# A hybrid diffusion block on one core: layer norms in two parts, context tokens first

## What is computed

```python
def half_ffn(x, shift, scale, gate, w_in, w_out, g, b):
    h = modulate(x, shift, scale)                    # x * (1 + scale) + shift
    a, u = jnp.split(h @ w_in, 2, axis=-1)           # (1024, 2 * 2816)
    y = (jax.nn.silu(a) * u) @ w_out                 # (2816, 1024)
    return layernorm(ALPHA * x + 0.5 * gate * y, g, b)
```

## Time and profile before

| | |
|---|---|
| three runs | 3256.19, 3259.68, 3264.73 us, median 3259.68 |
| profiled execution | 3258.92 us, its span 3257.2 us |
| busy: PE, PEld, DVE, ACT, POOL | 93%, 76%, 49%, 26%, 7% of the span |
| mean granted TensorE clock | 0.969 |
| DMA | 269 MB, mean 83 GB/s |

### The profile page before, as it was taken

One profiled execution on the slowest core, in us unless ns is written; L12 is line 12 of the kernel. 1 busy time (PEld: TensorE's weight loads), 2 busy tenths in 40 slices (PEclk: granted clock), 3 DMA queues, 4 the chain that ended last, 5 costly groups with the idle time before them and its releaser, 6 DMA issues.

```text
span 3257.2 us, 41934 instructions
## 1 busy us (share of the span) xinstructions
PE 3040.4 (93%) x16507; PEld 2489.4 (76%) x16507; DVE 1582.5 (49%) x2391; ACT 842.5 (26%) x1262; POOL 237.8 (7%) x351
## 2 busy tenths in 40 slices
PE   5999999999976989999999899999996998899997
PEld 2588888877843768888887788888865897688785
DVE  3434344445456464343434644444354887454544
ACT  0411111124244141111112411111143665322221
POOL 1000000000010001010100000000001653000000
PEclk8999999999988999999999999999998999999998
DMA  7344432201121224343420222212111110133330
GB/s 284 104 146 138 131 114 65 65 27 52 52 69 53 65 78 155 116 154 117 154 91 26 65 65 64 59 60 61 39 47 46 28 26 14 52 116 90 90 92 38
DMA packets 292648, 269.32 MB, mean 83 GB/s; under 512 B 31111, under 2 KB 257263, under 8 KB 292432
## 3 DMA queue, kind: packets, MB, share of 16 engines
q1 hardware_dynamic: 269936, 188.95, 19.5%
q0 software_dynamic: 21760, 76.03, 6.7%
q10 hardware_dynamic: 864, 3.15, 0.3%
HBM read 262.85 MB, written 5.24 MB: 82 GB/s over the span
## 4 chain that ended last, share of the span: by engine, by line
PE 86%; DVE 6%; ACT 5%; issue 1%; DMA 1%; POOL 1%; SPq 0%; ACTq 0%; DVEq 0%; POOLq 0%
PE PSALL L1912 25%; PE PSALL L1913 24%; PE PSALL L1914 24%; PE PSALL L1833 2%; PE PSALL L2009 1%; PE PSALL L2260 1%; ACT H L810 1%; PE PSALL L2245 1%; PE PSALL L1875 1%; ACT HHI L813 1%; PE PSALL L2124 1%; DVE RSTD L1447 1%; ACT SQ L883 1%; PE PSALL L2099 1%; DVE X L1452 1%
## 5 line engine op out<-in xcount | busy, mean ns | idle before, releaser
L1912 PE MATMUL PSALL<-HHI,WHIA 128*128 128x512 f32 (+1 forms) x1520 | 536.6, 353 | 48.0 <-DVE HLO L1335 39.9
L1913 PE MATMUL PSALL<-HLO,WHIA 128*128 128x512 f32 (+1 forms) x1520 | 527.8, 347 | 0.0
L1914 PE MATMUL PSALL<-HHI,WLOA 128*128 128x512 f32 (+1 forms) x1520 | 527.0, 347 | 0.0
L1912 PE MATMUL PSALL<-HHI,WHIB 128*128 128x512 f32 (+1 forms) x1488 | 512.0, 344 | 10.8 <-DVE WLOB L1238 10.8
L1913 PE MATMUL PSALL<-HLO,WHIB 128*128 128x512 f32 (+1 forms) x1488 | 512.0, 344 | 0.0
L1914 PE MATMUL PSALL<-HHI,WLOB 128*128 128x512 f32 (+1 forms) x1488 | 511.2, 344 | 0.0
L1386 DVE SCALAR_TENSOR_TENSOR X<-PSALL,GATE,X 128x512 f32<-128x512 f32 (+1 forms) x616 | 376.1, 633 | 242.1 <-PE PSALL L1914 239.6
L1912 PEld LDWEIGHTS PSALL<-HHI,WHIA 128*128 128x128 f32 x1520 | 290.5, 191 | 113.3 <-issue 40.6
L1914 PEld LDWEIGHTS PSALL<-HHI,WLOA 128*128 128x128 f32 x1520 | 291.1, 192 | 35.6
L1912 PEld LDWEIGHTS PSALL<-HHI,WHIB 128*128 128x128 f32 x1488 | 281.9, 189 | 45.3 <-issue 8.5
L1913 PEld LDWEIGHTS PSALL<-HLO,WHIA 128*128 128x128 f32 x1520 | 291.8, 192 | 31.5
(11 more groups left out here) (265 smaller groups left out, 4279.9 us busy)
## 6 DMA issues: line engine op xcount, KB each, us to landing
RAW<-in_ffn_w_in_dram SPq DMA_DIRECT2D x176, 512.0 KB, 4.2
ADA<-in_ada_w_dram POOLq DMA_DIRECT2D x144, 512.0 KB, 4.9
RAW<-in_ffn_w_out_dram SPq DMA_DIRECT2D x88, 512.0 KB, 3.5
RAW<-in_ev_w_in_dram SPq DMA_DIRECT2D x20, 512.0 KB, 4.2
WRAW<-in_mla_w_q_up_dram SPq DMA_DIRECT2D x16, 288.0 KB, 3.0
RAW<-in_ev_w_out_dram SPq DMA_DIRECT2D x8, 512.0 KB, 4.8
RAW<-in_mla_w_in_dram SPq DMA_DIRECT2D x8, 512.0 KB, 4.2
RAW<-in_mla_w_out_dram SPq DMA_DIRECT2D x8, 512.0 KB, 4.6
```

The source lines that it names most:

```text
L1912: te.matmul(out, w_hi, x_hi(k), start=(k == 0), stop=False)
L1913: te.matmul(out, w_hi, x_lo(k), start=False, stop=False)
L1914: x = te.matmul(out, w_lo, x_hi(k), start=False, stop=(k == ks - 1))
```

## The change

1. `ORDER = {2: (1, 0), 1: (0,)}`: in a norm over both kinds the context is part a = 0, the latents part a = 1; h, residual and all counts follow.
2. `last_down`: the last down projection takes the eight context chunks, then the eight latent chunks, through other PSUM banks. The sums of a chunk (`sum_chunk`) stand two chunks later, and the context's variance after latent chunk 4.
3. `first_pair`: A and B of the next stage together. Chunk by chunk over the context: half 0 of A and of B; then the latents' variance; then half 1 over the context; then A's latents (both halves for each chunk as it comes), then B's.
4. `next_unit`: B's weights are split ahead of the norm's end, as A's.
5. `even_out` and `odd_out` replace `project` for the output projections, with sums between their products; in `even_out` units 2 and 3 take the context first.
6. The tables of coefficients (`tables`) go into the last FFN loop body; the SP queue's wait ahead of the rope tables now names the count of the norm before.

```diff
 # ScalarE, layernorm (S is 2 with context, 1 without)
+            if nxt:
+                next_unit(nxt, "A")
+            mean(0)
+            for m in range(KC):
+                square(0, m)
+            if nxt:
+                next_unit(nxt, "B")
+            root(0)
+            if name == "final":
+                return
+            if S == 2:
+                for m in range(3):
+                    h(0, m)
+                mean(1)
+                for m in range(KC):
+                    if m + 3 < KC:
+                        h(0, m + 3)
+                    square(1, m)
+                root(1)
+            for m in range(KC):
+                h(S - 1, m)
...
 # VectorE
+        def ctx_end(name):
+            for m in range(3, KC):
+                norm(name, 2, 0, m)
+                ln_low(name, 2, 0, m - 2)
+                if m >= 5:
+                    center(name, 2, 1, m - 5)
+            for m in (6, 7):
+                ln_low(name, 2, 0, m)
+                center(name, 2, 1, m - 3)
+            for m in range(5, KC):
+                center(name, 2, 1, m)
+        def ln_end(name, S):
+            a = S - 1
+            inverse(name, S, a)
+            norm(name, S, a, 0)
+            for m in range(KC):
+                if m + 1 < KC:
+                    norm(name, S, a, m + 1)
+                ln_low(name, S, a, m)
...
 # VectorE, end of an ffn
-            for e in range(KC * S):
-                accumulate(FI - 1, e)
+            next_unit(nxt, "A")
+            for m in range(KC):
+                last_chunk(1, m)
+            last_chunk(0, 0)
+            for m in range(4):
+                center(then, 2, 0, m)
+            last_chunk(0, 1)
+            for m in range(4, KC):
+                center(then, 2, 0, m)
+            for m in (2, 3, 4):
+                last_chunk(0, m)
+            next_unit(nxt, "B")
+            last_chunk(0, 5)
+            inverse(then, 2, 0)
+            last_chunk(0, 6)
+            for m in range(3):
+                norm(then, 2, 0, m)
+            ln_low(then, 2, 0, 0)
+            last_chunk(0, 7)
+            ctx_end(then)
...
 # VectorE, end of ev_out
+            for m in range(4, KC):
+                out_chunk("ev_out", 2, 1, 1, m, 4)
+            next_unit("ffn1", "A")
+            out_chunk("ev_out", 2, 1, 0, 4, 5)
+            for m in range(KC):
+                center("ln1", 2, 0, m)
+            out_chunk("ev_out", 2, 1, 0, 5, 6)
+            next_unit("ffn1", "B")
+            inverse("ln1", 2, 0)
+            for m in range(3):
+                norm("ln1", 2, 0, m)
+            out_chunk("ev_out", 2, 1, 0, 6, 5)
+            ln_low("ln1", 2, 0, 0)
+            out_chunk("ev_out", 2, 1, 0, 7, 6)
+            ctx_end("ln1")
...
 # TensorE, last_down
+                for m in range(KC):
+                    if m >= 4:
+                        te.wait_ge(evac, e0 + m - 3)
+                    chunk(1, m, last_bank(1, m))
+                    if m >= 2:
+                        sum_chunk(then, 2, 0, m - 2, e0 + m - 1)
+                for m in range(KC):
+                    if m >= 2:
+                        te.wait_ge(evac, e0 + KC + max(0, m - 3))
+                    chunk(0, m, last_bank(0, m))
+                    if m == 0:
+                        for k in (6, 7):
+                            sum_chunk(then, 2, 0, k, e0 + k + 1)
+                    if m >= 2:
+                        sum_chunk(then, 2, 1, m - 2, e0 + KC + m - 1)
+                    if m == 4:
+                        variance(then, 2, 0)
+                for m in (6, 7):
+                    sum_chunk(then, 2, 1, m, e0 + KC + m + 1)
...
 # TensorE, first_pair; columns() waits for h_lo chunk by chunk, at chunk 0 of part 0 for both slots' lo_done
+            if S == 2:
+                columns(0, [(slot, 0) for slot in "AB"])
+                if ln != "h0":
+                    variance(ln, 2, 1)
+                columns(0, [(slot, 1) for slot in "AB" if halves[slot] > 1])
+            for slot in "AB":
+                columns(S - 1, [(slot, half) for half in range(halves[slot])])[slot].then_inc(pe[slot], done[slot])
...
 # TensorE, even_out (after units 0 and 1)
+            for n, slot in enumerate("AB"):
+                te.wait_ge(evac, p.evac + 4 * (n + 1))
+                for half in range(2):
+                    x = unit_product("ev_out", slot, p.q + 4 + 2 * n, half, 1, order)
+                x.then_inc(pe[slot], 1)
+                for m in range(0, 4) if n == 0 else (4, 5):
+                    sum_chunk("ln1", 2, 0, m, p.evac + (8 if m < 4 else m + 5))
+            unit_product("ev_out", "A", p.q + 4, 0, 0, order).then_inc(pe["A"], 1)
+            for m in (6, 7):
+                sum_chunk("ln1", 2, 0, m, p.evac + m + 5)
+            for m in (0, 1):
+                sum_chunk("ln1", 2, 1, m, p.evac + 8)
+            unit_product("ev_out", "A", p.q + 4, 1, 0, order).then_inc(pe["A"], 1)
+            for m in (2, 3, 4):
+                sum_chunk("ln1", 2, 1, m, p.evac + (8 if m < 4 else 13))
+            variance("ln1", 2, 0)
+            unit_product("ev_out", "B", p.q + 6, 0, 0, order).then_inc(pe["B"], 1)
+            sum_chunk("ln1", 2, 1, 5, p.evac + 14)
+            unit_product("ev_out", "B", p.q + 6, 1, 0, order).then_inc(pe["B"], 1)
+            for m in (6, 7):
+                sum_chunk("ln1", 2, 1, m, p.evac + m + 9)
```

More of the change, by code:

```diff
@@ L457, in down_bank, with last_bank, stat_bank @@
         return PS[6 + m % 2][:, 0:LAT] if s == 0 else PS[5][:, CTX * (m % 2):CTX * (m % 2) + CTX]
+    LAST_CTX, LAST_LAT = (1, 2, 4, 5), (6, 7, 2, 1)
+    def last_bank(s, m):
+        return PS[(LAST_LAT if s == 0 else LAST_CTX)[m % 4]][:, 0:SEGS[s][1]]
+    STAT_BANKS = {"ln0": (3, 0), "ln1": (7, 6), "ln2": (3, 0), "ln3": (3, 0), "ln4": (6,), "final": (0,)}
+    def stat_bank(name, s):
+        return PS[STAT_BANKS[name][s]][:, 0:SEGS[s][1]]
     block = stack.enter_context(nc.Block())
@@ L857, in body @@
                     split_hi(slot, half, p.q + j, i, free_value(slot, i + d))
-            body(0, first=True)
+            silus("A", 0)
+            for slot, d, half, j in ffn_halves(False)[2:]:
+                split_hi(slot, half, p.q + j, 0, free_value(slot, d))
             if ada:
@@ L1006, in in_split @@
                 before = [0, 0, 3, 2, 5][u]
[L1007 to L1018, removed]
+                for half in range(2):
+                    split_hi(slot, half, p.q + MLA_HALF[u] + half, 0, base + before)
             for u in range(5):
@@ new lines, in ffn @@
+            if S == 1:
+                for e in range(KC):
+                    accumulate(FI - 1, e)
+                for m in range(KC):
+                    center(then, 1, 0, m)
+                return
+            next_unit(nxt, "A")
[7 more added lines that the diff above has]
+                center(then, 2, 0, m)
@@ L1467, in even_mixer @@
+        ffn("ffn0", 2, 0, N_ADA - ADA_FIRST, ADA_FIRST, "ln0", "ev_in", lambda: tables(0))
+        ln_end("ln0", 2)
         def even_mixer():
@@ L1655, in _, with odd_out @@
+        def odd_out():
+            for u in range(4):
+                for half in range(2):
+                    out_chunk("mla_out", 1, 4, 0, 2 * u + half, 2 * (u // 2) + half + 1)
+                if u < 2:
+                    out_split("mla_out", u + 2)
+                if u == 2:
+                    next_unit("ffn3", "A")
+            for m in range(KC):
+                center("ln4", 1, 0, m)
+            next_unit("ffn3", "B")
         even_mixer()
-        layernorm("ln1", 2, 2)
+        ln_end("ln1", 2)
@@ L1671, in odd_mixer @@
+        ln_end("ln3", 2)
         def odd_mixer():
@@ new lines, in odd_out @@
+        def odd_out():
+            p, order = plan["mla_out"], list(range(KC))
+            for u in range(4):
+                slot = "AB"[u % 2]
+                if u >= 2:
+                    te.wait_ge(evac, p.evac + 2 * (u - 1))
+                for half in range(2):
+                    wait = (lambda k, s: te.wait_ge(och_lo, k + 1)) if u == 0 and half == 0 else None
+                    unit_product("mla_out", slot, p.q + 2 * u, half, 0, order, wait, (OHI, OLO)).then_inc(pe[slot], 1)
+                if u >= 2:
+                    for m in range(4 * (u - 2), 4 * (u - 2) + 4):
+                        sum_chunk("ln4", 1, 0, m, p.evac + m + 1)
@@ L2134, in even_mixer @@
             te.wait_ge(hy_t, 2 * NF + 2 * HC)
-            project("ev_out", 2, 2, [4, 5, 6, 7, 0, 1, 2, 3], ready, evac, 4)
-        ffn("ffn0", 2, N_ADA - ADA_FIRST)
-        layernorm("ln0", 2)
+            even_out(ready)
+        ffn("ffn0", 2, N_ADA - ADA_FIRST, "h0", "ln0")
         even_mixer()
-        layernorm("ln1", 2, (6, 7))
-        ffn("ffn1", 2, N_ADA)
-        layernorm("ln2", 2)
-        ffn("ffn2", 2, 0)
-        layernorm("ln3", 2)
+        ffn("ffn1", 2, N_ADA, "ln1", "ln2")
```

512 lines of the change are left out of this document (267 added, 245 removed).

## The result

The kernel after takes 3266.44 us (median of 8 runs, 3265.00 to 3273.94), the kernel before 3257.32 in the same session (8 runs, 3254.83 to 3264.73): ratio 1.003, 95% interval 1.002 to 1.0039. It is slower, by 9 us. The profiled execution took 3269.34 (before 3258.92), so the traces differ by 10.4 us. The forecast was 3270, and +10.4 on the profiled execution. The profiled execution lies 2.9 us over the median of its own kernel.

A forecast was written before the change was run, and what follows sets the result against it. TensorE (PE) holds 86% of the chain, so only its idle or half-clock time around norms can give time; +2.0, +1.2, +9.0, -5.1, +5.6, -2.3 gave +10.4 on 3258.92, 3269.3; median forecast 3270, range 3255 to 3282.

The forecast's parts named there:

- six stretches: Where the change acts: h0 and ln0 to ln4, each ending with the next B unit; summed change +10.4 us.
- The rounds: ScalarE alternates context h and latent squares, VectorE low parts and centering: one chain, 2.67 us per round.
- ln0: Stretch from the first last-down matmul to the end of the next B unit: 82.2 to 83.4 us, +1.2.
- ln3: Norm stretch where B is the 64-row unit and only A has a second context half: 75.3 to 80.9, +5.6 us.
- ln2: Third norm's stretch, last down to first two up units: B's 4.1 us wait for its split goes, -5.1 us.
- Rival 1: The clock holds through the rounds, saving 2.2 us in four stretches: 3261; chance 0.14.
- ln1: Stretch from the third output unit to ffn1's B unit: PE waits 2.6 and 6.9 us for latent evictions, +9.0 us.
- h0: First stretch, context first: PE's first B group waits for B's low half, +2.0 us.
- ln4: Latents-only norm stretch: A runs both halves for each chunk as it comes, -2.3 us.
- Sums between groups at 0: On PE, sums moved between down groups cost 0; upper bound +3 us a stretch if weight loads were exposed.
- Rival 2: The rounds are not chains; center and square run ahead: 3243, or 3256 if only half comes; chance 0.12.
- Rival 3: Loop's first split late behind residual and gating, or sums expose weight loads: 3282; chance 0.16.

The follow-up runs named there:

- experiment 1: Kernel after, ScalarE's order changed in ln0 to ln3: h of context chunks 3 to 7 first, then the eight latent squares, instead of alternating; 3237.06 us.
- experiment 3: Kernel after, h0 only: PE takes both context halves of unit A, then both of B, instead of A and B per chunk; 3263.08 us.
- experiment 4: Kernel after, ten unneeded matmuls added behind the first context groups of chunks 2 to 6 in ln0, ln2 and ln3; 3263.09 us.
- Experiment 2: Kernel after, ln1 only: latent evictions ahead of the weight splits on VectorE, ScalarE's norm work ahead of the weight copies; 3253.33 us.
- Experiment 8: Kernel before, one edit: VectorE makes B's two low splits at the head of the residual instead of behind it; 3238.67 us.
- experiment 5: Kernel after with the edits of experiment 1, Experiment 2 and experiment 3 together; 3215.23 us.

## Why the prediction was right

**How much of the number is luck.** The traces differ by 10.4 us as forecast, but only 9.3 of it lies in the six stretches, and by the medians it is 9.1. The mechanism is shown; that the traces agree to a tenth is chance.

**The rounds (decisive step): right, shown.** The forecast laid one chain of 2.67 us; the trace has 2.66 to 2.67 in ln0 to ln3, and experiment 1 removes it by the written order alone. In ln0, counted from the first down matmul, the last low part came at 44.5 (forecast 43.4), the end of the variance at 53.8 (53.8), the latents at 61.5 (61.2), B's end at 83.8 (83.4).

**Two sizes in ln0 were off and cancelled.** I left out the half clock at the first down groups, although have it for ln2: three groups took 3.6 us, where I had 2.2 and a wait of 0.5. The kernel before has full clock there in ln0, and so has experiment 3, whose code is the same as that of the kernel after in this place: behind the same gap of 2.56 us it comes to the fourth chunk in 2.97 us instead of 3.97. So this 1.0 us comes and goes between executions, and no run here says why. And I took 2.2 for the half clock at the end of the rounds. The last group took 1.45 us and the variance 7.34; at full clock, in experiment 4, they take 0.82 and 6.46, so the half clock costs 1.5. My 6.87 for a variance at full clock was 0.4 too much as well. That the end of the variance fits to a tenth is luck. The clock fell two rounds earlier than I said, but there the half-speed groups lie inside waits and cost nothing; and it came back sooner, after 1.7 us of the variance.

**Rival 1 (the clock holds) was wrong.** In ln0 the clock fell to 0.50 at 734.0, behind the first of the rounds' waits of 1.69, 1.69, 1.02 and 1.01 us, none of them long, and stayed there for 10.2 us. Its price of 2.2 a stretch was too high: it is 1.5. The Trainium skill, "TensorE: Matmul & The Clock Gate", has two sections on this: "HAM oscillation — how this bites in real kernels" speaks of long single gaps, and by it the clock should have held; "A second HAM failure mode: psum-queue depth-cycling" speaks of frequent short idles between groups of matmuls, and this trace agrees with that one in so far as the idles are short (1.69 us and less); how frequent they have to be it does not show, as the clock fell behind the first. I weighed the first section alone.

**ln1: right, term by term.** Waits 2.54 and 7.06 (forecast 2.6 and 6.9). The stretch is 0.8 over the forecast. Experiment 2 shows the price of the two waits with their clock: 12.5 us in a stretch that lost 9.8. Without them ln1 is 2.7 us shorter than before the change.

**ln2: right, and for the reason given.** Experiment 8 gets 5.9 us in the kernel before with B's split alone. That the net of ln2, 6.0, is the same number is in part chance. In ln0, which never had this wait, the same change costs 1.6, so ln2 does better by 7.6: 5.9 is the wait, and 1.5 is the half clock at its first down groups, which in the kernel before ln2 had and ln0 had not (18.33 against 16.81 us to the first sum). Experiment 8 also says something that the forecast did not: this wait existed in ln1 and h0 as well, so 18.6 us could be had without the two-part norm, against the 42 of experiment 5 with it.

**ln3 1.2 us under the forecast**: A starts after an idle time of 4.26 us (forecast 4.4), but the end of the rounds cost 1 us less, as in ln0. For A at half clock I had 2.2; it took 12.6 us instead of 11.4, so 1.2 (in experiment 5, 13.6, so 2.2). My sum had another slip there: 62.4 + 11.3 + 2.2 is 75.9, not 75.5. **ln4 -2.3, h0 +1.8, final 0:** as forecast; PE's last wait is 12.76 us before and after.

**Sums between groups at 0: right.** In ln0 of the kernel after the sums of context chunks follow each other in steps of 1.14 us (702.03, 703.17, 704.31, 705.45), a down chunk of 0.72 and a sum of 0.43; those of the latents in 2.24, which is 1.37 and 0.87. No weight load shows.

**Rival 2 (no chains) did not hold for this order.** I priced a kernel without the chains at 3243. The one in which the two jobs no longer alternate, experiment 1, took 3237.

**Rival 3 (the loop's first split late) did not occur**, not even where PE is 50 us earlier in all: in experiment 5 PE has no wait of over 0.25 us in the first units behind h0, ln0, ln1 and ln2.

## What to carry to other kernels

Where two engines with in-order queues pass chunks of two jobs to each other, write down for one round which instruction each waits for; if every one of them waits for the other engine's last one, the round costs the sum of all four, and grouping by job instead of alternating cost nothing here. Before an early start of a next stage is built, look at the small waits that already stand there: one split moved ahead of a residual gave 18.6 us, twice what the whole change lost. Put work that needs no result of a chain where the chain runs, and evictions that PE waits for ahead of preparations for a later stage.

## What the runs showed of the hardware

In ln0 of the kernel after the granted clock fell from 2.4 to 1.2 GHz behind one wait of 1.69 us and a group of matmuls, and it stayed low for 10.2 us while waits of 1.69, 1.02 and 1.01 us followed. With the waits of the same rounds filled, so that none was over 0.49 us, it stayed at 2.4 GHz. A gap of 1.38 us ahead of the latents left it at 2.4 GHz in experiment 1. The same gap does not always have the same end: behind 2.56 us ahead of ln0's last down projection the clock fell in the kernel after and held in experiment 3; behind 4.25 or 4.26 us in ln3 unit A ran 5.6 us at 1.2 GHz in experiment 5, but only 3.4 in the kernel after. Behind 7.26 us (ln4, after) it was again 5.6. Filling the gaps of ln3 and ln4 with matmuls of no use gave back 2.2 us each, without delaying the work behind them.
